# Two hybrid layers and two mixer layers on one core: the odd block's gates, recurrence and GELUs at earlier units, top-k rounds in other head steps, and an attention mask in two short-format products

## The reference

```python
def hybrid_layer(x, ...):                       # twice
    x = x + 0.5 * swiglu(rmsnorm(x, ffn1_norm), ...)
    z = rmsnorm(x, mix_norm) @ w_in
    y_a = dsa_mixer(...)       # top-k of index scores, attention with a bias by distance
    y_b = gla_mixer(...)       # gated linear attention, chunks of 64
    y_c = conv_mixer(...)      # 31 taps
    y_d = mla_mixer(...)       # causal attention, 4 heads, rotary part of 32
    x = x + concat(y_a, y_b, y_c, y_d) @ w_out
    return x + 0.5 * swiglu(rmsnorm(x, ffn2_norm), ...)

def second_block(x, ...):
    for layer in range(2):
        hn = rms_norm(x, norm_mix_pre[layer])
        mix = even_mixer(hn, ...) if layer % 2 == 0 else odd_mixer(hn, ...)
        x = x + rms_norm(mix, norm_mix_post[layer])
        ff = swiglu_2(rms_norm(x, norm_ffn_pre[layer]), ...)
        x = x + rms_norm(ff, norm_ffn_post[layer])
    return x

def odd_mixer(xn, ...):
    z = xn @ w_in                                # 1024 x 2048
    xc = causal_conv(z[..., :1024], 4 taps)
    gate_r, gate_i = sigmoid(xc @ w_r + b_r), sigmoid(xc @ w_i + b_i)   # 4 blocks of 256
    log_a = -8 * gate_r * softplus(-lam)
    h = scan(exp(log_a), sqrt(-expm1(2 * log_a)) * (gate_i * xc))       # over the tokens
    return (h * gelu(z[..., 1024:])) @ w_out
```

## Time and profile before

| | before |
|---|---|
| median of 3 runs | 3483.84 us (3483.67 to 3484.84) |
| profiled execution | 3482.52 us |
| its span | 3480.7 us |
| TensorE busy | 3359.6 us, 97% |
| VectorE busy | 1595.7 us, 46% |
| ScalarE busy | 1170.0 us, 34% |
| GpSimd busy | 411.5 us, 12% |
| mean granted TensorE clock | 0.987 |

### The profile page before, as it was taken

How to read it: one execution, slowest core, us unless ns; L and a number is a source line. 1 busy time by engine, 2 the same in 40 slices (tenths; PEclk the granted TensorE clock), 3 DMA queues, 4 the chain that set the end, 5 groups by cost and what they waited for, 6 DMA issues and landing times.

```text
span 3480.7 us, 39701 instructions
## 1 busy us (share of the span) xinstructions
PE 3359.6 (97%) x14384; PEld 2578.8 (74%) x14384; DVE 1595.7 (46%) x2295; ACT 1170.0 (34%) x1726; POOL 411.5 (12%) x285
## 2 busy tenths in 40 slices
PE   7999999999999999999899999999999999899998
PEld 5888775778887788876677888565678886668886
DVE  3332489643323433288834331944343327643322
ACT  4332345432323332245533321214333214543322
POOL 1110002111100110000211100400111003111100
PEclk9999999999999999999999999999999999999999
DMA  4333231033333333332023333440223332223332
GB/s 138 93 94 97 85 79 50 3 89 96 91 96 91 90 96 92 95 79 75 1 64 88 96 92 95 99 76 31 65 86 96 93 94 85 61 79 90 96 94 76
DMA packets 420124, 286.04 MB, mean 82 GB/s; under 512 B 57416, under 2 KB 395180, under 8 KB 419884
## 3 DMA queue, kind: packets, MB, share of 16 engines
q1 hardware_dynamic: 419200, 283.62, 28.5%
q10 hardware_dynamic: 828, 1.13, 0.1%
HBM read 280.24 MB, written 4.47 MB: 82 GB/s over the span
## 4 chain that ended last, share of the span: by engine, by line
PE 90%; DVE 6%; ACT 2%; issue 2%; POOL 0%; DMA 0%; DVEq 0%; ACTq 0%; SPq 0%; POOLq 0%
PE bank L856 26%; PE bank L857 26%; PE bank L858 25%; PE bank L851 1%; PE bank L1147 1%; PE bank L1146 1%; PE bank L1165 1%; PE bank L1261 1%; PE bank L1267 1%; PE bank L1384 1%; DVE small L2257 1%; PE bank L996 0%; PE bank L998 0%; PE bank L997 0%; PE bank L1348 0%
## 5 line engine op out<-in xcount | busy, mean ns | idle before, releaser
L858 PE MATMUL bank<-xn_lo,w_hi 128*128 128x512 f32 x2800 | 1097.5, 392 | 0.0
L856 PE MATMUL bank<-xn_hi,w_hi 128*128 128x512 f32 x2496 | 1000.2, 401 | 42.8 <-DVE xn_lo L1973 20.1
L1984 DVE TENSOR_TENSOR w_lo<-wring,w_hi 128x1024 fp32r<-128x1024 f32 x478 | 594.5, 1245 | 926.0 <-ACT w_hi L1511 925.1
L857 PE MATMUL bank<-xn_hi,w_lo 128*128 128x512 f32 x2496 | 989.3, 396 | 0.0
L1511 ACT ACTIVATE w_hi<-wring 128x1024 fp32r<-128x1024 f32 x490 | 517.6, 1059 | 1194.7 <-DMA wring<-in_ffn_down 358.5
L858 PEld LDWEIGHTS bank<-xn_lo,w_hi 128*128 128x128 f32 x2800 | 528.7, 189 | 132.5
L856 PEld LDWEIGHTS bank<-xn_hi,w_hi 128*128 128x128 f32 x2496 | 470.0, 188 | 165.0 <-issue 49.4
L857 PEld LDWEIGHTS bank<-xn_hi,w_lo 128*128 128x128 f32 x2496 | 470.8, 189 | 104.6 <-issue 2.6
L857 PE MATMUL bank<-h_hi,w_lo 128*128 (+1 forms) x1056 | 420.4, 398 | 0.0
L856 PE MATMUL bank<-h_hi,w_hi 128*128 (+1 forms) x1056 | 415.8, 394 | 0.0
L858 PE MATMUL bank<-h_lo,w_hi 128*128 (+1 forms) x1056 | 415.2, 393 | 0.0
(11 more groups left out here) (382 smaller groups left out, 2913.7 us busy)
## 6 DMA issues: line engine op xcount, KB each, us to landing
wring<-in_ffn_gate SPq DMA_DIRECT2D x88, 512.0 KB, 3.8
wring<-in_ffn_up SPq DMA_DIRECT2D x88, 512.0 KB, 3.8
wring<-in_ffn_down SPq DMA_DIRECT2D x88, 512.0 KB, 3.5
wring<-in_ffn_w_gate SPq DMA_DIRECT2D x44, 512.0 KB, 3.8
wring<-in_ffn_w_up SPq DMA_DIRECT2D x44, 512.0 KB, 3.8
wring<-in_ffn_w_down SPq DMA_DIRECT2D x44, 512.0 KB, 3.5
wring<-in_w_in SPq DMA_DIRECT2D x34, 512.0 KB, 3.7
wring<-in_w_out SPq DMA_DIRECT2D x16, 512.0 KB, 3.6
```

The lines of the kernel that those rows point to most:

```text
L856: nc.tensor.matmul(ps, w_hi[:, slot, t, 0:M], hi, start=start, stop=False)
L857: nc.tensor.matmul(ps, w_lo[:, slot, t, 0:M], hi, start=False, stop=False)
L858: return nc.tensor.matmul(ps, w_hi[:, slot, t, 0:M], lo, start=False, stop=stop)
L1984: nc.vector.tensor_tensor(w_lo[:, slot, :, :].rearrange("p k c -> p (k c)"), wunit[:, slot, :], w_hi[:, slot, :, :].rearrange("p k c -> p ...
```

## The change

It has three parts.

- *Last attention.* In each head the query blocks now run downwards, from `tb` = 3 to 0. The table `lnmult` is split once, into `ln_hi` (ScalarE) and `ln_lo` (VectorE), the identity is copied into the short format (`one_r`, ScalarE), and the mask is added as two short-format products, one_r x ln_hi and one_r x ln_lo, instead of one fp32 product. The start of the attention also waits for the split.
- *Odd block.* The gate products stand behind units 5, 6, 8 and 9; tanh and exp behind 6 and 10; square roots behind 9 and 12; squares behind 8 and 12; scans behind 10 and 13. Five GELUs are issued behind unit 13, one behind 14, one ahead of the loop that makes `xn_hi` and one inside it. VectorE gates five tiles and splits two weight units between the pick-ups of units 14 and 15, and gates the other three inside its last loop.
- *Head steps.* The rounds of the top-k in steps 0 to 8 go from 2, 2, 1, 1, 1, 1, 1, 1, 1 to 2, 2, 2, 2, 1, 0, 0, 0, 0, and `END_ROUNDS` from 4 to 6. The rotary part of the four keys moves from VectorE to GpSimd, behind GpSimd's other products there, and ScalarE's norm of head vector u waits for it from u = 5 on. The mask of a diagonal block stands ahead of the chunk.

Beside these, the semaphore `fin_ps` goes, and the last transposes count on `pro_ps`.

```diff
@@ -212,8 +212,9 @@
...
 DMA_ODD = [USE_ODD // 2] * 2
-GATES_AT = {5: 0, 7: 1, 9: 2, 11: 3}
+GATES_AT = {5: 0, 6: 1, 8: 2, 9: 3}
 LRU_HALF = 4
+GEL_LOOP = 6
@@ -451,6 +452,9 @@
...
         rope_t = [T(32), T(33)]
+        ln_hi, ln_lo = [nc.alloc_sbuf_tensor_at(n, [P, SEQ], F32R, offset=at["arena"] + t * SEQ * 4)
+                        for n, t in (("ln_hi", 22), ("ln_lo", 23))]
+        one_r = nc.alloc_sbuf_tensor_at("one_r", [P, P], F32R, offset=at["arena"] + 24 * SEQ * 4)
@@ -1140,11 +1144,13 @@
...
                     q, k = ops["qk"](m, h)
-                    msk, lo = ops["mask"](m, h, tb, i)
+                    masks, lo = ops["mask"](m, h, tb, i)
...
                     nc.tensor.matmul(s[:, lo:N], q[:, tb * P:N], k[:, lo:N], start=True, stop=False)
-                    nc.tensor.matmul(s[:, lo:N], ident, msk, start=False, stop=True).then_inc(att_s.h, 1)
+                    for n, (one, msk) in enumerate(masks):
+                        mm = nc.tensor.matmul(s[:, lo:N], one, msk, start=False, stop=(n == len(masks) - 1))
+                    mm.then_inc(att_s.h, 1)
@@ -1183,10 +1189,10 @@
...
             if m == "D":
-                return C("causal"), tb * P
+                return [(ident, C("causal"))], tb * P
             if tb == 0:
-                return bias[:, h, SEQ - P:SEQ], 0
-            return T(t_bm[BM.index(u) % 3])[:, 0:(tb + 1) * P], 0
+                return [(ident, bias[:, h, SEQ - P:SEQ])], 0
+            return [(ident, T(t_bm[BM.index(u) % 3])[:, 0:(tb + 1) * P])], 0
@@ -1204,7 +1210,7 @@
...
             if m == "D" and tb == 0:
-                eng.e.wait_ge(dh_ready.h, dh_ready.by(eng.l, h + 1))
+                eng.e.wait_ge(dh_ready.h, dh_ready.by(eng.l, 5 + h))
@@ -1221,7 +1227,7 @@
...
-        E_UNITS = [("E", h, tb) for h in range(E_HEADS) for tb in range(TB)]
+        E_UNITS = [("E", h, tb) for h in range(E_HEADS) for tb in reversed(range(TB))]
@@ -1231,13 +1237,17 @@
...
                 eng.e.wait_ge(glu_sb.h, 4)
+                eng.e.wait_ge(ln_split.h, 1)
             m, h, tb = E_UNITS[u]
-            if tb == 0 and h % 2 == 0:
+            if tb == TB - 1 and h % 2 == 0:
...
-        EVEN = dict(qk=even_qk, mask=lambda m, h, tb, u: (C("lnmult")[:, SEQ - (tb + 1) * P:], 0),
+        def even_mask(m, h, tb, u):
+            return [(one_r[:, :], t[:, SEQ - (tb + 1) * P:]) for t in (ln_hi, ln_lo)], 0
+
+        EVEN = dict(qk=even_qk, mask=even_mask,
@@ -1636,9 +1646,9 @@
...
                     act.e.wait_ge(dn_ps.h, dn_ps.by(act.l, u + 1))
-                    if 2 <= u < 6:
+                    if u >= 2:
                         act.e.wait_ge(dh_ready.h, dh_ready.by(act.l, u - 1))
-                    elif u >= 6:
+                    if u >= 6:
@@ -1660,6 +1670,7 @@
...
             nc.scalar.preload_act_table_set(LN_EXP)
+            act.e.wait_ge(dh_ready.h, dh_ready.by(act.l, 8))
@@ -1804,6 +1815,8 @@
...
                     nc.scalar.activation(s5_yt[i % 2], pb[7][:, :], ACT.Gelu_apprx_tanh).then_inc(s5_gelu.h, 1)
+            nc.scalar.activation(one_r[:, :], ident, ACT.Copy)
+            nc.scalar.activation(ln_hi[:, :], C("lnmult"), ACT.Copy).then_inc(tab_sin.h, 1)
@@ -1854,6 +1867,11 @@
...
+        def act_gelu(act, k):
+
+            act.e.wait_ge(oz_sb.h, KD + k + 1)
+            nc.scalar.activation(T(o_gel + k), T(o_gel + k), ACT.Gelu_apprx_tanh).then_inc(og_sb.h, 1)
+
@@ -1861,17 +1879,22 @@
...
                     act_gates(act, GATES_AT[n])
-                if n in (7, 11):
-                    act_decay(act, (n - 7) // 4)
-                if n in (10, 14):
-                    act_sqrt(act, (n - 10) // 4)
+                if n in (6, 10):
+                    act_decay(act, (n - 6) // 4)
+                if n in (9, 12):
+                    act_sqrt(act, (n - 9) // 3)
+                if n == 13:
+                    for k in range(GEL_LOOP - 1):
+                        act_gelu(act, k)
+                if n == 14:
+                    act_gelu(act, GEL_LOOP - 1)
             act_units(act, then, 0, 2)
-            for k in range(KD):
-                act.e.wait_ge(oz_sb.h, KD + k + 1)
-                nc.scalar.activation(T(o_gel + k), T(o_gel + k), ACT.Gelu_apprx_tanh).then_inc(og_sb.h, 1)
+            act_gelu(act, GEL_LOOP)
...
                     act.e.wait_ge(unit_ps.h, st.units + 2 * KD)
+                if k == 3:
+                    act_gelu(act, GEL_LOOP + 1)
@@ -2153,9 +2176,9 @@
...
         HEAD_TOP = sum(Z_ROUNDS)
-        HEAD_ROUNDS = [2, 2, 1, 1, 1, 1, 1, 1, 1]
+        HEAD_ROUNDS = [2, 2, 2, 2, 1, 0, 0, 0, 0]
         HEAD_END = HEAD_TOP + sum(HEAD_ROUNDS)
-        END_ROUNDS = 4
+        END_ROUNDS = 6
@@ -2215,16 +2238,13 @@
...
                     col = RL["d_k_norm"]
-                    if i == 4:
-                        dve.e.wait_ge(mn_x.h, mn_x.by(dve.l, 9))
...
                                                    scalar=cur[0:D_NOPE, col:col + 1], in1=T(t_hr[i % 2])[0:D_NOPE, :],
-                                                   op0=ALU.mult, op1=ALU.mult)
-                    nc.vector.tensor_tensor(T(t_dk[i - 4])[64:96, :], k_rot, T(t_hr[i % 2])[64:96, :], ALU.mult).then_inc(dn_x.h, 1)
+                                                   op0=ALU.mult, op1=ALU.mult).then_inc(dn_x.h, 1)
+                if 4 <= i < 8:
+                    dve_inside(dve, i - 4)
...
                     dve_chunk(dve, i - 1)
-                if i >= 4 and i < 8:
-                    dve_inside(dve, i - 4)
@@ -2548,6 +2568,8 @@
...
                     tt(t, t, rope_t[u % 2], ALU.add).then_inc(rot_ready.h, 1)
+            dve.e.wait_ge(tab_sin.h, 5)
+            tt(ln_lo[:, :], C("lnmult"), ln_hi[:, :].bitcast(F32), ALU.subtract).then_inc(ln_split.h, 1)
@@ -2576,17 +2598,27 @@
...
-            st = STAGES["in", "odd"]
+            def gated(k):
+                dve.e.wait_ge(o_h.h, k + 1)
+                dve.e.wait_ge(og_sb.h, 2 * KD + k + 1)
+                tt(T(o_xc + k), T(o_xc + k), T(o_gel + k), ALU.mult).then_inc(y_lru.h, 1)
+
+            st, then = STAGES["in", "odd"], STAGES["out", "odd"]
...
                 tt(dst, pb[IN_BANKS[n % 4]][:, :], gain_r, ALU.mult).then_inc(oz_sb.h, 1)
-                if n in (10, 14):
-                    squares((n - 10) // 4)
-                if n in (11, 15):
-                    scans((n - 11) // 4)
+                if n in (8, 12):
+                    squares((n - 8) // 4)
+                if n in (10, 13):
+                    scans((n - 10) // 3)
+                if n == 14:
+                    for k in range(GEL_LOOP - 1):
+                        gated(k)
+                    dve.e.wait_ge(u_lo.h, then.units)
+                    dve_units(dve, then, 0, 2)
@@ -2602,17 +2634,13 @@
...
-            then = STAGES["out", "odd"]
-            dve_units(dve, then, 0, 2)
-            for k in range(KD + 1):
-                if k < KD:
-                    dve.e.wait_ge(o_h.h, k + 1)
-                    dve.e.wait_ge(og_sb.h, 2 * KD + k + 1)
-                    tt(T(o_xc + k), T(o_xc + k), T(o_gel + k), ALU.mult).then_inc(y_lru.h, 1)
-                if k:
-                    dve.e.wait_ge(xn_hi_ready.h, then.splits * KD + k)
-                    tt(xn_lo[:, k - 1, :], T(o_xc + k - 1), xn_hi[:, k - 1, :].bitcast(F32), ALU.subtract).then_inc(xn_lo_ready.h, 1)
-                    dve_units(dve, then, k + 1, min(k + 2, SLOTS))
+            for k in range(KD):
+                dve.e.wait_ge(xn_hi_ready.h, then.splits * KD + k + 1)
+                dve.e.wait_ge(y_lru.h, k + 1)
+                tt(xn_lo[:, k, :], T(o_xc + k), xn_hi[:, k, :].bitcast(F32), ALU.subtract).then_inc(xn_lo_ready.h, 1)
+                if k < KD - GEL_LOOP + 1:
+                    gated(GEL_LOOP - 1 + k)
+                dve_units(dve, then, k + 2, min(k + 3, SLOTS))
@@ -2721,6 +2749,12 @@
...
                 nc.gpsimd.tensor_tensor(dst, dst, T(t_hr[u % 2])[0:D_QK, :], ALU.add).then_inc(dh_ready.h, 1)
+            pool.e.wait_ge(mn_x.h, mn_x.by(pool.l, 9))
+            for u in range(4, 8):
+                pool.e.wait_ge(dn_r.h, dn_r.by(pool.l, u + 1))
+                pool.e.wait_ge(dh_ready.h, dh_ready.by(pool.l, u))
+                nc.gpsimd.tensor_tensor(T(t_dk[u - 4])[64:96, :], k_rot, T(t_hr[u % 2])[64:96, :], ALU.mult).then_inc(dh_ready.h, 1)
+            pool.e.wait_ge(dh_ready.h, dh_ready.by(pool.l, 8))
```

8 lines of the change are left out of this document (4 added, 4 removed).

## The result

| | before | changed |
|---|---|---|
| median of 4 runs | 3484.34 us (3483.67 to 3485.78) | 3506.13 us (3501.92 to 3508.77) |
| profiled execution | 3482.52 us | 3506.84 us |
| its span | 3480.7 us | 3505.1 us |
| TensorE busy | 3359.6 us | 3395.7 us |
| mean granted TensorE clock | 0.987 | 0.975 |

A forecast was written before the change was run, and what follows sets the result against it. TensorE, busy 97% of the span, was taken as the bound. Gains of 9.4 (last attention), 3.5 (odd block) and 4.4 us (head steps) sum to 17.3: 3466.5 us beside the median of 3483.84, range 3457.5 to 3476.5.

The forecast's parts named there:

- Part 1, the work: Last attention: cheaper mask products give 7.5 us, shorter waits 2.7 and 1.2, less 2 of new waits: 9.4 us gain.
- rival (a): Last attention's mask: narrow short-format products no cheaper than fp32; total gain only 2.3 us, 3481.5; chance 0.08.
- a product that costs its columns alone: Last attention's mask, upper bound: narrow products have no minimum time, so the part gains 15 us.
- the floor of 0.11 us: Last attention's mask: no short-format product takes less than the 0.11 us of a transpose with its own weights.
- The waits of 0.34 us: Last attention: TensorE's wait for an earlier unit's scaling, one a head, 2.7 us, goes with blocks running downwards.
- Part 1, the clock: Last attention: new TensorE waits, from successive weight splits on VectorE and ScalarE, counted as 2 us of loss.
- the rival: This is rival (d): the granted clock falls in the last attention; chance 0.03.
- Part 2: Odd block: VectorE's chain behind the last input product ends at 3022.2 instead of 3025.74, a gain of 3.5 us.
- Part 3: Head steps, both hybrid layers: shorter wait for att_diag, VectorE still the bound into the attention; 4.4 us gain in all.
- the term of 2.2 us a layer: Head steps: four rotary products leaving VectorE save 3.8 us, GpSimd's stops cost 1.6; TensorE gets the 2.2 left.
- rival (d): Last attention: granted clock falls to 1.2 GHz; whole gain gone from 17 us of such work, up to 3533; chance 0.03.
- Rival (b): Odd block and head steps: GpSimd's stops of VectorE eat these gains; 7 us gain in all, 3477; chance 0.12.

The follow-up runs named there:

- p1: Kernel before with only the last attention's part (short-format mask, query blocks downwards): 3474.67 us against 3485.67; run again unaltered, 3473.97 against 3485.80.
- after_spread: Changed kernel with ScalarE's and VectorE's weight splits in the last attention at every fourth step instead of four in a row: 3477.56 us, kernel before 3484.62.
- p2: Kernel before with only the odd block's part of the change: 3480.63 us against 3485.67.
- p3_rounds: Kernel before with only the head steps' new top-k rounds (six at the end), rotary products left on VectorE: 3480.37 us against 3484.74.
- all_warm: Changed kernel with weight splits at every fourth step and three unread fp32 products in TensorE's wait for att_diag: 3468.44 us, kernel before 3484.74.
- p3_warm: Kernel before with the head steps' part and three unread fp32 products in TensorE's wait for att_diag: 3485.59 us against 3484.74.
- p3: Kernel before with only the head steps' part, in both hybrid layers: 3493.56 us against 3485.67.
- p1_mask: Kernel before with only the last attention's short-format mask, query blocks upwards as before: 3477.33 us against 3485.67.
- p1_shift: p1 with one fp32 GLU product ahead of the last attention made five times more: 3506.94 us, kernel before 3485.80.

## Why the prediction was wrong

**Part 1, the work: right, a little small.** The pairs were put at 0.28, 0.34, 0.45 and 0.55 us; they took 0.27 (2389.69 to 2389.96), 0.34, 0.45 and 0.56. So neither rival (a) nor a product that costs its columns alone: the floor of 0.11 us holds in this format, 0.11 us being what the second product of 128 columns took. The waits of 0.34 us are gone, but I had counted eight of them, 2.7 us, where the trace of the kernel before has six, 2.0 us. And nearly all of the 2 us of new waits that I had set against them is missing: one came, of 0.92 us. In `p1` the part gave 11 to 12 us against 9.4.

**Part 1, the clock: this step failed.** I counted the new waits as 2 us at their own length. The one that came, 0.92 us, was followed by a loss of some 29 us in the executions in which the clock fell to the end (3503 against 3474 us in `p1`; 17.8 us lost against 11.7 gained over the attention, in the traces of the changed kernel and of `after_spread`). I had the rival, with its price: past 17 us of work at the lower level the gain is gone. There were 64 us at half the clock, so 32 us of such work. What was wrong was its chance. My reason against it was that the clock was 1.00 over all 80.5 us and that the waits get fewer. Fewer they are, yet one came that is longer than the 0.34 us of a head before, and it could have been found: I named VectorE's and ScalarE's four splits in successive steps, and added VectorE's work to 9.3 us a round, but never laid ScalarE's instructions of step 13 end to end: copies, split, exponential, scaling. Nor did I ask how near the old waits of 0.34 and 1.17 us had come to a fall.

**Part 2: right.** 3.5 us was predicted; the odd block gave 4.2 us in the trace of the changed kernel and 4.0 in that of `p2`, whose median is 5.0 us lower. VectorE's row in the changed kernel, from the stopped scan to the split for the output product:

```profile
3018.16 3.31 DVE L2599 TENSOR_TENSOR_SCAN arena<-arena 128x512 f32<-128x512 f32 x1
...
3028.65 4.70 DVE L2588 SCALAR_TENSOR_TENSOR cst<-arena,cst 128x512 f32<-128x512 f32 x4
3033.28 0.68 DVE L2612 TENSOR_TENSOR arena<-bank,scratch 128x512 f32<-128x512 f32 x1
...
3044.25 3.09 DVE L2604 TENSOR_TENSOR arena<-arena 128x512 f32<-128x512 f32 x5
3047.25 2.35 DVE L2007 TENSOR_TENSOR w_lo<-wring,w_hi 128x1024 fp32r<-128x1024 f32 x2
3049.53 0.68 DVE L2612 TENSOR_TENSOR arena<-bank,scratch 128x512 f32<-128x512 f32 x1
3050.13 0.68 DVE L2640 TENSOR_TENSOR xn_lo<-arena,xn_hi 128x512 fp32r<-128x512 f32 x1
```

The trace lies 28.8 us late here, so the last row stands at 3021.3 on the old scale, where I had 3022.2. Both stops by GpSimd came, one in the scan and one in the squares, at the size of the row they were taken from.

**Part 3: the wait was right, the term of 2.2 us a layer and what follows it failed.** The wait for `att_diag` was to go from 5.4 to "near 3 us or less"; it is 2.9. But VectorE's gain was mis-sized. Its rounds end at 613.19 in the changed kernel, 1.2 us earlier than before (613.39) when the lag of 1.0 us is taken off, not 2.2: the moved products and their stops were in the sum, the wait of 1.61 us for ScalarE's norm was not. And even the 1.2 us did not reach TensorE, whose gain I had put equal to VectorE's: VectorE then waits 2.11 us for TensorE. The sum has no term for the clock at which TensorE makes the products behind the wait. In the kernel before the first 32 ran at half the clock and the 28 behind them at the full one; in the changed kernel the 28 were slow too. The one stretch at a lower clock that I named there, 636 to 638, I used for rival (d) alone. And the saving of 2.2 us rested on the four moved products; the rounds, which I costed at nothing ("the rounds ahead of the last mask are nine before and nine after"), gave 4.4 us by themselves in `p3_rounds`, 2.6 us of it where a short fall is missing, and the products are the piece that makes the loss likely. That 4.4 is also the forecast for this part is luck: the reason was another. Rival (b) had the products' cost as stops of VectorE. They are there, a gain of 1.85 us instead of 0.73 for one, but that is not where most of the time went.

With TensorE's clock held (`all_warm`) the three parts together gain 16.3 us, near the 17.3 of the sum. That is not the sum come true: part 1 gives more there than it says, and part 3 by itself nothing (`p3_warm` at +0.9).

**What stays open.** Beside these parts, the GLU ahead of the last attention lost 1.7 us in the changed kernel to one more short fall, behind a wait of 1.9 us that both kernels have. Why a fall ends after 20 us in one execution and goes on for 64 in another, with the same work in both, no run shows. Nor does one show where the clock fell in the long executions of `p3` and `p1_mask`. And whether it is position alone that raises the share from 4 in 18 to 9 in 14 between `p1` and the changed kernel was not tried by itself. `p1_shift` points to it, but its five products are also more work for TensorE ahead of the attention, and the two weren't told apart. Six executions against eighteen are few.
